# A swiglu stage whose products take both halves at once, and weight tiles whose low halves are made by an adding transfer

## What is computed

```python
D_FF = -(-8 * D_MODEL // (3 * 256)) * 256          # 2816
...
        h2 = modulate_2(rmsnorm_2(x, g_ffn[l]), mod[:, 3, None], mod[:, 4, None])
        x = x + mod[:, 5, None] * swiglu(h2, w_up[l], w_down[l])
    return rmsnorm_2(x, g_final)
```

## Time and profile before

| | |
|---|---|
| median of three runs | 908.47 us (906.63 to 911.72) |
| span of the profiled execution, first to last instruction | 903.1 us |
| the profiled execution's own time | not listed; the median less the span is 5.4 us |
| PE busy | 884.7 us (98%) |
| DVE, ACT, POOL busy | 710.0, 504.7, 142.2 us |
| moved by the weight queue of SP | 147.73 MB |
| moved by GpSimd's queue | 46.61 MB |
| mean granted TensorE clock | 0.996 |

### The profile page before, as it was taken

One profiled execution on the slowest core, in us unless ns is written; L12 is line 12 of the kernel. 1 busy time (PEld: TensorE's weight loads), 2 busy tenths in 40 slices (PEclk: granted clock), 3 DMA queues, 4 the chain that ended last, 5 costly groups with the idle time before them and its releaser, 6 DMA issues.

```text
span 903.1 us, 17404 instructions
## 1 busy us (share of the span) xinstructions
PE 884.7 (98%) x7132; PEld 829.2 (92%) x7132; DVE 710.0 (79%) x1033; ACT 504.7 (56%) x727; POOL 142.2 (16%) x254
## 2 busy tenths in 40 slices
PE   8999999999999999999999999999999999999996
PEld 6688776689999999989999999999999999999995
DVE  5689667989888999968569975797987998765543
ACT  5474888997845455225554465483535644444441
POOL 0003864710021001300211100300001000000000
PEclk9999999999999999999999999999999999999998
DMA  9946987885776677866638844555556567666661
GB/s 365 388 144 216 306 271 222 280 274 181 214 276 210 230 262 269 293 215 201 184 103 292 303 128 142 178 173 187 155 180 181 172 204 255 187 185 183 196 204 52
DMA packets 55295, 195.45 MB, mean 216 GB/s; under 512 B 7856, under 2 KB 7984, under 8 KB 53808
## 3 DMA queue, kind: packets, MB, share of 16 engines
q1 hardware_dynamic: 39600, 147.73, 50.4%
q0 software_dynamic: 15616, 46.61, 15.2%
HBM read 188.60 MB, written 1.05 MB: 210 GB/s over the span
## 4 chain that ended last, share of the span: by engine, by line
PE 75%; DVE 14%; ACT 4%; issue 3%; DMA 2%; POOL 1%; DVEq 0%; SPq 0%; ACTq 0%; POOLq 0%
PE ps L582 22%; PE ps L584 21%; PE ps L583 21%; DVE w_lo L1415 4%; PE ps L756 3%; PE ps L685 2%; PE px L674 2%; ACT w_hi L980 1%; DVE win L1429 1%; DVE dump L1788 1%; DMA x<-in_xT 1%; DMA raw<-in_stream 1%; DVE li L1429 1%; PE px L861 1%; DVE li L1614 1%
## 5 line engine op out<-in xcount | busy, mean ns | idle before, releaser
L1415 DVE TENSOR_TENSOR w_lo<-raw,w_hi 128x1024 fp32r<-128x1024 f32 x232 | 280.5, 1226 | 83.9 <-ACT w_hi L980 83.3
L980 ACT ACTIVATE w_hi<-raw 128x1024 fp32r<-128x1024 f32 x232 | 242.7, 1055 | 110.8 <-DMA raw<-in_stream 110.0
L582 PE MATMUL ps<-h_hi,w_hi 128*128 128x256 f32 (+1 forms) x864 | 256.0, 296 | 6.2 <-DVE w_lo L1415 2.8
L583 PE MATMUL ps<-h_lo,w_hi 128*128 128x256 f32 (+1 forms) x864 | 251.4, 291 | 0.0
L584 PE MATMUL ps<-h_hi,w_lo 128*128 128x256 f32 (+1 forms) x864 | 251.3, 291 | 0.0
L582 PEld LDWEIGHTS ps<-h_hi,w_hi 128*128 128x128 f32 x864 | 165.3, 191 | 16.6 <-issue 5.7
L583 PEld LDWEIGHTS ps<-h_lo,w_hi 128*128 128x128 f32 x864 | 165.4, 191 | 3.5 <-issue 1.2
L584 PEld LDWEIGHTS ps<-h_hi,w_lo 128*128 128x128 f32 x864 | 165.4, 191 | 2.7
L459 POOL DMA_DIRECT2D modw<-in_mod_w x80 | 42.8, 536 | 391.6 <-DVE modw L1449 250.1
L582 PE MATMUL ps<-h2o_hi,w_hi 128*128 128x256 f32 x352 | 101.5, 288 | 0.0
L584 PE MATMUL ps<-h2o_hi,w_lo 128*128 128x256 f32 x352 | 99.6, 283 | 0.0
(11 more groups left out here) (353 smaller groups left out, 1856.6 us busy)
## 6 DMA issues: line engine op xcount, KB each, us to landing
raw<-in_stream SPq DMA_DIRECT2D x252, 512.0 KB, 3.8
modw<-in_mod_w POOLq DMA_DIRECT2D x80, 512.0 KB, 5.7
m<-in_mod_w SPq DMA_DIRECT2D x8, 1024.0 KB, 19.5
shifts<-upad POOLq DMA_DIRECT2D x128, 35.5 KB, 4.7
c_row<-in_c_rows SPq DMA_DIRECT2D x3, 512.0 KB, 7.6
ctxT<-in_ctxT SPq DMA_DIRECT2D x1, 1024.0 KB, 4.9
x<-in_xT SPq DMA_DIRECT2D x1, 1024.0 KB, 7.1
ctx2T<-in_ctx2T SPq DMA_DIRECT2D x1, 1024.0 KB, 6.5
```

Of the source, the lines that this page charges most:

```text
L582: pe.matmul(o, wh, hi, start=start, stop=False)
L583: pe.matmul(o, wh, lo, start=False, stop=False)
L980: act.activation(w_hi[split[0] % HI_RING][:], raw[n % RING][:], ACT.Copy).then_inc(w_hi_ready, 1)
L1415: v.tensor_tensor(w_lo[n % RING][:], raw[n % RING][:], w_hi[split[0] % HI_RING][:].bitcast(F32), ALU.subtract).then_inc(w_lo_ready, 1)
```

## The change

Two things are done in the stage at the end.

The first: where the activation's halves lie behind each other in memory (`h3_both`, `ff_both`), one product of 512 columns multiplies the high weight by both (`two_columns`). It leaves high by high in the first half of the bank and high by low in the second, and a product of 256 columns adds low by high to the first half. The two halves are summed afterwards. In up this is done from t = 12 on (`UP_WIDE`): ScalarE copies the second half out (`second_half`), VectorE adds the first, ScalarE takes the Silu in SBUF, VectorE multiplies. In down it is done for t = 0 to 6, where VectorE adds both halves to x one after the other.

The second: for the 14 tiles `ua 8` to `ua 21` and the 8 tiles `d0` (`ADDED`) VectorE no longer subtracts. ScalarE writes the negated high half into `w_lo`, and GpSimd issues a transfer that adds the raw tile, read from the stream again, to it. PE waits for that transfer.

```diff
+UP_WIDE = 12
...
+ADDED = [n for n in HALVED if ORDER[n][0] in ("ua", "d0") and n >= TILE[("ua", 8)]]
+ADDED_NTH = {n: sum(m % RING == n % RING for m in ADDED[:i]) for i, n in enumerate(ADDED)}
...
@@ gpsimd, behind its loads of modulation weights
+            for i, n in enumerate(ADDED):
+                pool.wait_ge(w_neg_ready, i + 1)
+                pool.dma_start(w_lo[n % RING][:], ins["stream"][n], accum_op=ALU.add).then_inc(w_lo_in[n % RING], 16)
             add_up([(sq5[:, 0, :], sq5)], sq_ready, 5 * KT, KT - 1)
...
@@ tensor, split_weights
-                pe.wait_ge(w_lo_ready, NTH[n] + 1)
+                if n in ADDED_NTH:
+                    pe.wait_ge(w_lo_in[n % RING], 16 * (ADDED_NTH[n] + 1))
+                else:
+                    pe.wait_ge(w_lo_ready, LOW_NTH[n] + 1)
...
+            def two_columns(name, t, both, ready=None, tiles=KT, first=True, last=True):
+
+                wh, wl = split_weights(name, t)
+                o = bank_of(name, t) if first else psum_of(name, t)
+                for k in range(tiles):
+                    if ready is not None:
+                        pe.wait_ge(ready[0], ready[1] + k + 1)
+                    pe.matmul(o[:, :], wh[:, k, :], both(k), start=(first and k == 0), stop=False)
+                    mm = pe.matmul(o[:, 0:T], wl[:, k, :], both(k)[:, 0, :], start=False, stop=(last and k == tiles - 1))
+                mm.then_inc(tile_done, 1)
...
             for t in range(4, FT):
-                thirds("ua", t, *h3, ready=(h_ready, 3 * KT) if t == 4 else None)
-                thirds("ub", t, *h3)
-            for t in range(KT):
+                if t < UP_WIDE:
+                    thirds("ua", t, *h3, ready=(h_ready, 3 * KT) if t == 4 else None)
+                    thirds("ub", t, *h3)
+                else:
+                    two_columns("ua", t, lambda k: h3_both[:, :, k, :])
+                    two_columns("ub", t, lambda k: h3_both[:, :, k, :])
+            for t in range(KT - 1):
...
@@ scalar, highs
+                    if n in ADDED_NTH:
+                        act.wait_ge(w_hi_ready, split[0] + 1)
+                        act.activation(w_lo[n % RING][:], w_hi[split[0] % HI_RING][:].bitcast(F32), ACT.Copy, scale=-1.0) \
+                           .then_inc(w_neg_ready, 1)
...
@@ scalar, up
+            def second_half(n, name, t):
+
+                done(name, t)
+                if t >= UP_WIDE + 2:
+                    act.wait_ge(ff_ready, t - 1)
+                act.activation(second[:, n, t % 2, :], psum_of(name, t)[:, T:2 * T], ACT.Copy).then_inc(second_out, 1)
+
...
+                    second_half(0, "ua", t)
+                    emptied(act, "ua", t)
+                    act.activation(sa[:, t % 4, :], sa[:, t % 4, :], ACT.Silu).then_inc(silu_made, 1)
+                    second_half(1, "ub", t)
...
@@ vector, up
+                    done("ua", t)
+                    v.wait_ge(second_out, 2 * (t - UP_WIDE) + 1)
+                    v.tensor_tensor(sa[:, t % 4, :], psum_of("ua", t)[:, 0:T], second[:, 0, t % 2, :], ALU.add) \
+                     .then_inc(free_of("ua", t), 1)
+                    done("ub", t)
+                    v.wait_ge(second_out, 2 * (t - UP_WIDE) + 2)
+                    v.tensor_tensor(fr, psum_of("ub", t)[:, 0:T], second[:, 1, t % 2, :], ALU.add).then_inc(free_of("ub", t), 1)
+                    emptied(v, "ub", t)
+                    v.wait_ge(silu_made, t - UP_WIDE + 1)
+                    S.do(tt_(fr, fr, sa[:, t % 4, :], ALU.mult))
...
@@ vector, down
+                if t < KT - 1:
+                    ahead("d2", t)
+                    v.wait_ge(tile_done, TILE[("d2", t)] + 1)
+                    S.do(v.scalar_tensor_tensor(out=x[:, t, :], in0=psum_of("d2", t)[:, T:2 * T], scalar=gate3[:, t:t + 1],
+                                                in1=x[:, t, :], op0=ALU.mult, op1=ALU.add))
+                    S.sync()
                 add_to_x("d2", t, gate3)
```

More of the change, by code:

```diff
@@ L107 @@
 HI_RING = 6
+ADDED = [n for n in HALVED if ORDER[n][0] in ("ua", "d0") and n >= TILE[("ua", 8)]]
+ADDED_NTH = {n: sum(m % RING == n % RING for m in ADDED[:i]) for i, n in enumerate(ADDED)}
+LOW_NTH = {n: i for i, n in enumerate(n for n in HALVED if n not in ADDED_NTH)}
 MOD_TILES = KT + 3 * KT + 6 * KT
@@ L291, in build @@
         t4 = at("t4", W + 8, [KT, T])
-        h3_hi, h3_lo = at("h3_hi", W + 16, [KT, T], F32R), at("h3_lo", W + 24, [KT, T], F32R)
-        ff_hi, ff_lo = at("ff_hi", W + 32, [FT, T], F32R), at("ff_lo", W + 54, [FT, T], F32R)
+        h3_both = at("h3_both", W + 16, [2, KT, T], F32R)
+        h3_hi, h3_lo = h3_both[:, 0], h3_both[:, 1]
+        second = at("second", W + 96.25, [2, 2, T])
+        ff_both = at("ff_both", W + 32, [2, FT, T], F32R)
+        ff_hi, ff_lo = ff_both[:, 0], ff_both[:, 1]
         v4 = at("v4", W + 76, [2, T])
@@ L309, in build @@
         w_hi_ready, w_lo_ready = sem("w_hi_ready"), sem("w_lo_ready")
+        w_neg_ready = sem("w_neg_ready")
+        w_lo_in = [sem(f"w_lo_in{j}") for j in range(RING)]
         tile_done = sem("tile_done")
@@ L956, in _ @@
             for t in range(4, FT):
-                thirds("ua", t, *h3, ready=(h_ready, 3 * KT) if t == 4 else None)
-                thirds("ub", t, *h3)
-            for t in range(KT):
+                if t < UP_WIDE:
[5 more added lines that the diff above has]
+            for t in range(KT - 1):
+                for n, name in enumerate(("d0", "d1", "d2")):
+                    two_columns(name, t, lambda k: ff_both[:, :, n * KT + k, :], tiles=min(KT, FT - n * KT), first=(n == 0),
+                                last=(n == 2), ready=(ff_ready, n * KT) if t == 0 else None)
+            for t in range(KT - 1, KT):
                 for n, name in enumerate(("d0", "d1", "d2")):
                     thirds(name, t, lambda k: ff_hi[:, n * KT + k, :], lambda k: ff_lo[:, n * KT + k, :],
-                           tiles=min(KT, FT - n * KT), first=(n == 0), last=(n == 2),
-                           ready=(ff_ready, n * KT) if t == 0 else None)
+                           tiles=min(KT, FT - n * KT), first=(n == 0), last=(n == 2))
             two_chunks(px[0], sq5, 8, 6 * KT)
@@ L1391, in _ @@
                         h3_high(n)
[L1392 to L1395 removed]
+            def second_half(n, name, t):
[3 more added lines that the diff above has]
+                act.activation(second[:, n, t % 2, :], psum_of(name, t)[:, T:2 * T], ACT.Copy).then_inc(second_out, 1)
+            for t in range(4, FT):
+                if t < UP_WIDE:
+                    done("ua", t)
+                    act.wait_ge(ff_ready, t - 3)
+                    act.activation(sa[:, t % 4, :], psum_of("ua", t)[:, 0:T], ACT.Silu).then_inc(free_of("ua", t), 1)
+                else:
+                    second_half(0, "ua", t)
+                    emptied(act, "ua", t)
+                    act.activation(sa[:, t % 4, :], sa[:, t % 4, :], ACT.Silu).then_inc(silu_made, 1)
+                    second_half(1, "ub", t)
             root_table()
@@ L1413, in lows @@
                     n = HALVED[split[0]]
-                    v.wait_ge(w_hi_ready, split[0] + 1)
-                    v.tensor_tensor(w_lo[n % RING][:], raw[n % RING][:], w_hi[split[0] % HI_RING][:].bitcast(F32),
+                    split[0] += 1
+                    if n in ADDED_NTH:
+                        continue
+                    v.wait_ge(w_hi_ready, split[0])
+                    v.tensor_tensor(w_lo[n % RING][:], raw[n % RING][:], w_hi[(split[0] - 1) % HI_RING][:].bitcast(F32),
                                     ALU.subtract).then_inc(w_lo_ready, 1)
-                    split[0] += 1
             def ahead(name, t, by=4):
```

15 lines of the change are left out of this document (10 added, 5 removed).

## The result

The changed kernel takes 950.91 us (944.13 to 955.16, four runs) against 910.1 us for the kernel before beside it: a ratio of 1.0476, 95% interval 1.0434 to 1.0517. It is slower, as forecast, but by 41 us between the medians (43 by the ratio) and not by 12, and lies outside the forecast's range, 913 to 934. The profiled execution is the fastest of the four, 944.13 us, so its trace shows a little less than the median's loss.

What follows compares the result with a forecast made beforehand. TensorE was taken to bound the kernel, with no idle time from 700 us on. The terms -4.2 + 12.0 + 1.5 + 1 + 2 gave +12.3 us, so 908.5 became 920.8 us, range 913 to 934.

Steps and rivals of the forecast that it cites:

- 314 wide products: In up (160) and down (154): each 512-column product saves 0.0133 us over two narrow ones, a gain of 4.2 us.
- first wait: Ahead of ua 8 in up: its transfer, issued at 754.5, lands at 761.5; TensorE stands still for 12.0 us.
- half clock behind it: After the stall at ua 8 TensorE restarts at half speed, costing 1.5 us (bounds 0 and 4).
- later waits in up and down: Added tiles after the first come late by 1 us in up (0 to 4) and 2 in down (0 to 5).
- I take a middle between the two: Later added tiles: a value between no lateness and late links, 1 us in up, 2 us in down.
- x: Time of an adding transfer from issue to landing, put between 4.7 and 9.3 us; 7 taken for ua 8.
- two cases for the traffic: Up moves three tiles per 5.55 us (283 GB/s, no lateness), or four counting the added read (378 GB/s, links late).
- D: End of the tile six places before an added one, when the added tile's raw load starts.
- the first rival: Transfers that add are slow all along, x 9 or more in every case: +30, 938 us; chance 0.17.
- the four-tile case: Added read counts as a fourth tile in up, 378 GB/s: up's links up to 1 us late, down's 0.7 to 2.
- the second rival: The first added tile, ua 8, isn't late, so the kernel is faster: 904 to 907 us; chance 0.04.
- Nothing in the change moves this: In up: GpSimd's last modulation load stays issued at 753.93, since ScalarE's extra negations before it fall into idle time.

Runs made afterwards that it cites:

- e1: The changed kernel without adding transfers, VectorE making all low halves again, so wide products alone: 904.45 us, ratio 0.9977 to the kernel before.
- e2: The changed kernel with every product narrow again, so the 22 adding transfers alone: 944.85 us, ratio 1.0418 to the kernel before.
- e4: The changed kernel with adding transfers beginning at ua 12 instead of ua 8, 18 instead of 22: 932.71 us, ratio 1.0258 to the kernel before.
- e5: The changed kernel with GpSimd issuing the transfers for ua 8 to ua 10 ahead of its last modulation loads: 938.55 us, ratio 1.035.
- e9: The changed kernel with adding transfers for the eight d0 tiles alone, wide products kept: 921.02 us, ratio 1.0163 to the kernel before.
- e7: The kernel of e1 plus 16 adding transfers into used modulation buffers that nothing waits for: 904.55 us, ratio 0.9976 to the kernel before.
- e11: The changed kernel with adding transfers for ua 12, 14, 16, 18 and 20 alone: 907.86 us, ratio 1.0018 to the kernel before.

## Why the prediction was wrong

The forecast for the trace was +12.3 us, measured were +39.2. Term by term:

| term | forecast | measured |
|---|---|---|
| 314 wide products | -4.2 | -2.1 (e1) |
| first wait | 12.0 (9.7 to 14.3) | 15.1 |
| half clock behind it | 1.5 | 2.0 |
| later waits in up and down | 3 (0 to 9) | 6.1 + 10.2 |
| half clock behind those | not in the sum | 7.9, what is left (6.4 of it read directly) |

**Where it was right.** The direction, and why: no gain from VectorE's relief; GpSimd's order puts the transfer for ua 8 behind its last modulation load; PE waits from 749 on, falls to half clock, and nothing later gives it back; nothing is lost to summing the halves. e1, e2, e4 and e5 show these one by one.

**The step that failed** is "I take a middle between the two", with 1 us in up and 2 in down. The formulas for a late tile, x over 7.3 in up and over 6.2 in down, were good. But I had two cases for the traffic, priced both, and took a value between them, where one alone could be true. With an addition that counts twice, the raw loads land in 5.2 us and x is 7.7 (7 to 7.8 by stretch). The chain in the prediction's form is then D + 5.2 + 2.3 + x = D + 15.2: 1.3 late in up, where four links make 5, and 2.7 late in down, where three make 8. Measured: 6.1 and 10.2, over even the high ends of my two terms, 4 and 5, since raw loads took 5.2 and not 4.6. With 31.4 us of waits in place of 15 the result lies outside the range before the next point is counted: -2.1 + 31.4 + 2.0 = +31, 940 us.

The mechanism is that of the first rival, to which I gave 0.17: reading and adding fill the DMA engines, and raw loads land late as well. Its condition, an x of 9 or more in every case, didn't come true; the median is 7.7. Its 938 us was short of the result, mainly by the next point. (The prediction says that by the Trainium skill's page the four-tile case would hold, "which is the second rival". The four-tile case is the high one of its own forecast, and near to it stands the first rival, not the second, which is the one that comes out faster.)

**A term that was missing**: short waits can cost half clock too, 7.9 us in all. Behind one of 2.3 us that ended at 829.4 in the changed kernel:

```profile
826.00:828.00 2.00, 1.08 (x7) 0.67 (x5) 0.02 (x1) 0.42 (x1) 0.38 (x1) 1.00 1.28 340
828.00:830.00 2.00, 0.60 (x3) 0.56 (x4) 0.00 (x0) 0.43 (x1) 0.00 (x0) 1.00 0.81 193
830.00:832.00 2.00, 2.00 (x10) 1.71 (x9) 1.34 (x2) 1.97 (x4) 0.00 (x0) 0.61 1.03 272
832.00:834.00 2.00, 2.00 (x8) 1.71 (x8) 1.36 (x4) 0.93 (x1) 0.78 (x1) 0.54 0.44 150
834.00:836.00 2.00, 2.00 (x14) 1.72 (x13) 0.42 (x1) 1.38 (x3) 0.09 (x1) 1.00 0.56 61
```

PE was idle for 2.3 us, and then worked at 0.61 and 0.54 for 4 us. A pair of products took 0.64 us there instead of 0.353:

```profile
830.65 0.63 PE L620 MATMUL ps<-h_both,w_hi 128*128 128x512 f32 x1
831.08 0.41 PE L621 MATMUL ps<-h_both,w_lo 128*128 128x256 f32 x1
831.29 0.63 PE L620 MATMUL ps<-h_both,w_hi 128*128 128x512 f32 x1
```

Read in this way, the products behind four of the eight waits (2.3, 3.4, 3.0 and 2.8 us) lost 1.5 to 1.6 us each, 6.4 in all; those behind a wait of 2.2 us at 795 lost 0.1. The clock doesn't fall behind each wait of that length: in e9 a wait of 3.4 us that ended at 843 left it at 1.00, and the next, of 4.0, was followed by 0.50 for some 6 us:

```profile
844.00:846.00 2.00, 2.00 (x13) 1.77 (x12) 0.00 (x0) 0.45 (x1) 0.00 (x0) 1.00 0.96 203
...
864.00:866.00 2.00, 2.00 (x8) 1.71 (x7) 0.00 (x0) 2.00 (x4) 0.86 (x1) 0.50 0.02 6
```

I had priced the clock for the long wait alone.

**Sizes that were off.** The first wait: the last modulation load, at 753.93 before, is issued at 755.90 in the changed kernel. POOL's timeline of the changed kernel, then of e1:

```profile
755.90 0.53 POOL L469 DMA_DIRECT2D modw<-in_mod_w  x1 [8.56 <-DVE modw L1502]
756.41 2.71 POOL L518 DMA_DIRECT2D w_lo<-in_stream  x3
```
```profile
739.31 0.57 POOL L469 DMA_DIRECT2D modw<-in_mod_w  x1 [37.24 <-DVE modw L1502]
...
756.09 0.53 POOL L469 DMA_DIRECT2D modw<-in_mod_w  x1 [7.17 <-DVE modw L1502]
```

The last of the four loads starts 17.0 us behind the first in the changed kernel and 15.0 before. That is no effect of the adding transfers: in the seven runs that have the program of before up to this place (e1, e4, e7 to e11) it is 15.3 to 17.5 (16.8 in e1), and in e2, which has them, 15.2, with a first wait of 12.8. So "Nothing in the change moves this" isn't refuted; but I took the moment from one trace, and it scatters by 2.5 us. What moves it in one execution and not in another stays open. The transfer then took 8.07 us, not 7, and landed at 764.5.

The wide product: I took its price from a stage in which every product is wide. Here each stands between narrow ones and costs 0.233 us instead of 0.2267. And the 5.4 us between span and median weren't work outside the span: in the runs of the changed kernel the time is 1.8 us above the span. The rest is the difference between executions: the three runs behind the median lie between 906.63 and 911.72.

**What stays open**: why a wide product costs 0.006 us more between narrow ones; whether the full DMA engines or the second read at its source sets the 209 GB/s; why the clock fell behind some of the short waits and not behind others; and the 1.5 us of the 7.9 that aren't found behind the four waits.

## What to carry to other kernels

Work that is moved off an engine with idle time gains nothing, and the place that it goes to must be priced as a chain: load, each step, issue, landing, against the time that the ring gives. An adding transfer kept the DMA engines as busy as two loads do: count it twice in the traffic, and see whether the sum comes near what the engines can move. When a cost has two possible prices that lead to different states (covered, or late at each link), put a chance on each and don't average them; and where TensorE has no idle time add the half clock that may follow a wait: behind those of 1.8 to 4.5 us here it was mostly about 1.6 us, at times nothing and at most 2.9 (e9).

A transfer that is put at the end of an in-order queue starts when the last instruction ahead of it is through, however early its data is ready; compare that moment with the first use.

## What the runs showed of the hardware

- An adding transfer of 512 KB from GpSimd: 0.86 us to issue (a copy 0.53), 7.7 us to landing (a copy 4.9 to 5.6), and the DMA engines full at 209 GB/s, the added tile counted once (plain loads 410 to 436).
- Weights loaded for each product, fp32r: 0.120 us from start to start with 256 columns, 0.2267 with 512, 0.353 for a pair of both.
- TensorE's granted clock was 0.50 when it started again behind a wait of 15.1 us and was 1.00 again 4.5 us later; it was 0.54 to 0.61 for 4 us behind a wait of 2.3 us, and stayed at 1.00 behind one of 3.4 us in e9.
- In traces with the same program up to the changed stage, the time ahead of it differed by up to 12 us, while the length behind it agreed within 0.2 us in the three without waits for tiles.
